# Where the weight buffers of an fp32r matmul kernel begin, modulo 256 bytes

## What is computed

```python
# first block
mx = silu(c) @ ada_w + ada_b                      # modulation; the same for ctx
hx, hc = modulate(rmsnorm(x)), modulate(rmsnorm(ctx))
ux, uc = hx @ w_in, hc @ w_in                     # 1024 x 5120
ox = hgrn_bidir(ux, states from uc)               # gated scans in two directions
y = (sigmoid(..)*(fourier_mix(ux) @ w_a) + sigmoid(..)*(readout(ox) @ w_b)) @ w_out
x = x + mx2 * y
x = x + mx5 * ((silu(conv(h2 @ ffn_up)[:2816]) * conv(..)[2816:]) @ ffn_down)
# second block
p = rms_norm(x) @ w_in_2                          # 1024 x 2560
x = x + concat(band attention, short conv, pooling) @ w_out_2
x = x + square(relu(rms_norm(x) @ w_mlp1)) @ w_mlp2   # 1024 x 4096 and back
```

## Time and profile before

| | |
|---|---|
| median of 3 executions | 764.5 us (764.06 to 765.53) |
| profiled execution, device time | 764.52 us |
| its span, first to last instruction | 762.5 us |
| TensorE busy | 739.1 us, 97% of the span |
| VectorE / GpSimd / ScalarE busy | 491.2 / 398.5 / 358.6 us |
| mean granted TensorE clock | 0.993 |

### The profile page before, as it was taken

One profiled execution on the slowest core, in us unless ns is written; L12 is line 12 of the kernel. 1 busy time (PEld: TensorE's weight loads), 2 busy tenths in 40 slices (PEclk: granted clock), 3 DMA queues, 4 the chain that ended last, 5 costly groups with the idle time before them and its releaser, 6 DMA issues.

```text
span 762.5 us, 14142 instructions
## 1 busy us (share of the span) xinstructions
PE 739.1 (97%) x5852; PEld 717.0 (94%) x5852; DVE 491.2 (64%) x907; ACT 358.6 (47%) x452; POOL 398.5 (52%) x223
## 2 busy tenths in 40 slices
PE   7779999999999989999999999999899999999998
PEld 3679889999999989999999999999899999999997
DVE  3877797569526559777777764548655656556553
ACT  5586224245434555554555546346454433334331
POOL 0767553546648957878878877766585300000000
PEclk9999999999999989999999999999999999999999
DMA  9984886337534437555455544433435464464411
GB/s 362 417 360 162 344 304 262 140 111 244 207 110 159 166 117 294 177 188 200 167 170 199 184 167 166 166 112 111 148 133 203 181 220 165 169 216 160 176 57 56
DMA packets 21089, 145.84 MB, mean 191 GB/s; under 512 B 2465, under 2 KB 2977, under 8 KB 3746
## 3 DMA queue, kind: packets, MB, share of 16 engines
q1 hardware_dynamic: 20880, 144.87, 51.8%
q10 hardware_dynamic: 146, 0.07, 0.0%
HBM read 143.88 MB, written 1.05 MB: 190 GB/s over the span
## 4 chain that ended last, share of the span: by engine, by line
PE 90%; DVE 4%; ACT 4%; issue 2%; DMA 0%; DVEq 0%; ACTq 0%
PE bank L1426 24%; PE bank L1428 24%; PE bank L1427 24%; PE bank L1444 3%; PE CP L1428 2%; PE CP L1426 2%; PE CP L1427 2%; PE bank L1533 2%; PE bank L1469 1%; ACT SCR L793 1%; ACT whi L487 1%; PE bank L1484 1%; DVE GA L1119 1%; PE CP L1458 0%; PE bank L1642 0%
## 5 line engine op out<-in xcount | busy, mean ns | idle before, releaser
L469 POOL TENSOR_TENSOR wlo<-raw,whi 128x512 fp32r<-128x512 f32 (+1 forms) x201 | 377.8, 1910 | 170.6 <-ACT whi L487 170.5
L487 ACT ACTIVATE whi<-raw 128x2048 fp32r<-128x2048 f32 x103 | 196.3, 1907 | 43.7 <-PE bank L1428 29.2
L1186 DVE SCALAR_TENSOR_TENSOR Y<-bank,vec,Y 128x189 f32<-128x189 f32 (+2 forms) x352 | 123.0, 423 | 43.6 <-ACT Y L734 43.6
L1426 PE MATMUL bank<-H2h,whi 128*128 128x256 f32 x352 | 101.0, 287 | 1.7 <-DVE H2l L1161 1.7
L1427 PE MATMUL bank<-H2l,whi 128*128 128x256 f32 x352 | 100.6, 286 | 0.0
L1428 PE MATMUL bank<-H2h,wlo 128*128 128x256 f32 x352 | 99.8, 284 | 0.0
L1426 PE MATMUL bank<-H1h,whi 128*128 128x256 f32 (+1 forms) x288 | 90.9, 316 | 8.3 <-DVE H1l L917 4.5
L1428 PE MATMUL bank<-H1h,wlo 128*128 128x256 f32 (+1 forms) x288 | 89.2, 310 | 0.0
L1427 PE MATMUL bank<-H1l,whi 128*128 128x256 f32 (+1 forms) x288 | 89.0, 309 | 0.0
L850 DVE TENSOR_TENSOR wlo<-raw,whi 128x2048 fp32r<-128x2048 f32 x28 | 64.4, 2300 | 34.5 <-ACT whi L487 34.5
L1426 PE MATMUL bank<-H4h,whi 128*128 128x256 f32 x256 | 72.6, 284 | 0.0
(11 more groups left out here) (326 smaller groups left out, 1878.9 us busy)
## 6 DMA issues: line engine op xcount, KB each, us to landing
raw<-in_w_mlp SPq DMA_DIRECT2D x32, 1024.0 KB, 4.8
raw<-in_w_in SPq DMA_DIRECT2D x30, 1024.0 KB, 5.7
raw<-in_ffn_up SPq DMA_DIRECT2D x22, 1024.0 KB, 4.9
raw<-in_ada_hi SPq DMA_DIRECT2D x16, 1024.0 KB, 4.9
raw<-in_ffn_down SPq DMA_DIRECT2D x11, 1024.0 KB, 4.8
raw<-in_w_out SPq DMA_DIRECT2D x8, 1024.0 KB, 4.8
ada_s<-in_ada_s SPq DMA_DIRECT2D x4, 1024.0 KB, 18.1
ada_p<-in_ada_p SPq DMA_DIRECT2D x2, 1024.0 KB, 10.2
```

What stands on the lines that cost most here:

```text
L469: m = e.tensor_tensor(l[:, a:a + step], r[:, a:a + step], h[:, a:a + step].bitcast(F32), ALU.subtract)
L487: e.activation(whi[q % NHI][:, :], raw[n % NRAW][:, :], ACT.Copy).then_inc(s["w_hi"], 1)
L1186: e.scalar_tensor_tensor(o[:, r0:r1, c0:c1], z[:, r0 + dr:r1 + dr, c0 + dc:c1 + dc], cw[:, f, tap:tap + 1], o[:, r0:r1, c0:c1], ALU.mult, ...
L1426: e.matmul(out, h[:, col:col + P], xh, start=first, stop=False, skip_group_check=True)
```

## The change

`keep` gets a `lead`, a number of bytes left empty in front of a tile, and remembers where each tile lies. The three `whi` get leads of 192, 128 and 160 bytes, the three `wlo` leads of 224, 128 and 160. `base` is rounded up to a multiple of 1024. The tiles that borrow a weight buffer's space before it is first used (`ada_p`, `CROW`, `SQI`) are placed by the remembered offset instead of by the index. Nothing else differs: the instructions, their order on every engine and all semaphores are the same.

```diff
     start = 16512
     cursor = [start]
+    found = {}
...
-    def keep(name, shape, dt=F32):
+    def keep(name, shape, dt=F32, lead=0):
         size = int(np.prod(shape[1:])) * (1 if dt == U8 else 4)
+        cursor[0] += lead
+        found[name] = cursor[0]
         t = put(name, shape, dt, cursor[0])
...
-    whi = [keep(f"whi{i}", [P, CH], F32R) for i in range(NHI)]
-    wlo = [keep(f"wlo{i}", [P, CH], F32R) for i in range(NHI)]
+    whi = [keep(f"whi{i}", [P, CH], F32R, lead=(192, 128, 160)[i]) for i in range(NHI)]
+    wlo = [keep(f"wlo{i}", [P, CH], F32R, lead=(224, 128, 160)[i]) for i in range(NHI)]
...
-    base = cursor[0]
+    base = (cursor[0] + 1023) // 1024 * 1024
...
-    def at(t):
-        return (start + [*raw, *whi, *wlo].index(t) * CH * 4 - base) / 1024
+    def at(name):
+        return (found[name] - base) / 1024
...
-    CROW = area("CROW", [1, D], at(wlo[0]))
-    SQI = area("SQI", [P, KT, T], at(whi[2]))
+    CROW = area("CROW", [1, D], at("wlo0"))
+    SQI = area("SQI", [P, KT, T], at("whi2"))
```

More of the change, by code:

```diff
@@ L250, in build @@
     CBX = area("CBX", [P, D], 44)
-    def at(t):
-        return (start + [*raw, *whi, *wlo].index(t) * CH * 4 - base) / 1024
+    def at(name):
+        return (found[name] - base) / 1024
     ada_buf = {}
     for name, i, kb in (("ada_s", 0, 80), ("ada_s", 1, 48), ("ada_s", 2, 56), ("ada_s", 3, 88), ("ada_t", 2, 8),
-                        ("ada_t", 3, 24), ("ada_p", 0, at(whi[1])), ("ada_p", 1, at(wlo[2]))):
+                        ("ada_t", 3, 24), ("ada_p", 0, at("whi1")), ("ada_p", 1, at("wlo2"))):
         ada_buf[name, i] = area(f"{name}{i}", [P, CH], kb)
-    CROW = area("CROW", [1, D], at(wlo[0]))
-    SQI = area("SQI", [P, KT, T], at(whi[2]))
+    CROW = area("CROW", [1, D], at("wlo0"))
+    SQI = area("SQI", [P, KT, T], at("whi2"))
     TOK = area("TOK", [P, 2, D], 72)
```

## The result

The changed kernel takes 753.8 us (median of 4, 752.8 to 757.3), the kernel before 764.65 us beside it (764.1 to 765.5). The ratio is 0.9864 [0.9835, 0.9892]: faster by 1.4%, or 10.8 us, where 25.5 us were forecast. The direction was right, the forecast size more than twice what was measured, and, as the experiments show, the cause that I gave was wrong.

The account below looks back on a forecast made before the run. TensorE's start-to-start pace of matmuls was taken to bound the kernel. 764.5 us less 27.9 plus 1.4 and 1.0 gave 739 us, with 726 to 752 for this case and 724 to 778 for 8 in 10.

Parts of the forecast that it names:

- What bounds the kernel: Whole kernel: TensorE busy 97%, so the start-to-start distance of matmuls sets the time, whatever other engines do in SBUF.
- My reading: Matmul operands: a moving run beginning 32 past a multiple of 64 bytes costs 6.7 ns, such a load some 4 ns.
- The first rival: Matmul operands: weight-to-activation distance sets the pace and the new distances are worse; 775 us, from 767 to 786; chance 0.25.
- Pairs 0 and 1: Matmuls on the first two whi/wlo weight buffer pairs: aligned moving runs save 6.7 ns on 3168 matmuls, 21.2 us less.
- Pair 2: Matmuls on the third whi/wlo pair: load now 32 past a multiple of 64; 1584 matmuls, 4.3 us less.
- The 192 matmuls of 512 columns: Matmuls with two moving runs: 13.3 ns less for 143, 9.3 ns less for 49, together 2.4 us less.
- `by_tokens`: Its 288 matmuls, which load activations: 0.8 us less on pairs 0 and 1, 0.9 us more on pair 2, together nothing.
- The 1.4 us lost at the start: From 20 to 60 us, DMA engines 94% busy: at most 1.4 us of the gain does not arrive.
- The 1.0 us of the convolution: VectorE's convolution in the FFN stage: 1 us of waits at the stage's start, 3 us as the bad end.
- The holes: Empty bytes before weights, with XR, `con` and `vec` shifted: cost 0, with 1 us either way as bounds.
- The third: Matmul operands: distance matters and is better, one or two pairs falling; 757 us, from 750 to 762; chance 0.13.
- The second: Matmul pace: nothing changes with placement; 764.5 us, within 1 us; chance 0.20.

Follow-up runs that it names:

- e9: Changed kernel with weight-to-activation distances of 64 bytes on pairs 0 and 2 and 192 on pair 1; 745.8 us, 0.9758 of the kernel before.
- run 32: Not a follow-up run: words from "a moving run 32 past a multiple of 64", a stretch of moving operand beginning 32 bytes past such a multiple; no time.
- e1: Changed kernel with the six weight buffers and all activations 32 bytes lower, distances kept; 755.5 us.
- e2: Changed kernel with activations on a multiple of 1024 and all weight-to-activation distances back at 96 bytes; 765.15 us over 10 executions.
- e5: Changed kernel with all pairs at a weight-to-activation distance of 192 bytes; 756 us, executions from 748.9 to 759.7.
- e10: Changed kernel with weight-to-activation distances of 96 bytes in the FFN and second MLP and 192 in all other stages; 772.3 us.
- e12: Changed kernel with the distances of pairs 0 and 1 exchanged: 64, 192 and 160 bytes on pairs 0, 1 and 2; 751.8 us.
- e11: Changed kernel with weight-to-activation distances of 192 bytes on pairs 0 and 2 and 64 on pair 1; total time not given, FFN at 117.8, then 113.3 ns.
- e3: Changed kernel with weight-to-activation distances of 0, 32 and 128 bytes on pairs 0, 1 and 2; total time not given, paces 120.0, 116.7 and 118.8 ns.

## Where the prediction was right and which step failed

**What bounds the kernel: right.** Placement alone, with no instruction moved, took 2.4% off the time in e9, and the pace did not depend on the other engines.

**"My reading", the step that failed.** It took 6.7 ns for a moving run 32 past a multiple of 64 and 4 ns for a load. e1 and e2 give 0 for both with 256 columns: e1 puts the moving runs of all pairs 32 past such a multiple again and keeps the paces of 117.8 and 117.3 ns, e2 takes them off it and stays at 120.0. The evidence was the earlier trace rows against the earlier trace rows: 117.3 against 120.0 ns. I put that down to which operand was misaligned. It was the distance: 160 with the roles swapped, 96 without. The first rival's text had this very reading ("the loaded operand stands 96 bytes behind the moving one instead of in front of it"), and I set it aside because the excess grows with 512 columns. That argument was bad: no row showed how long a load reads beside the moving operand, and with 512 columns the pace follows the distance too, from 226.7 to 234.3 ns.

**The terms.** Pairs 0 and 1 were booked at 6.7 ns less, 21.2 us. They ran at 113.3 in stretches ahead of the FFN, but at 117.8 in the long stages: 2.2 ns, 7.0 us over the 3168 matmuls. Pair 2 at 117.3 came out to the tenth (4.3 us), which was luck: the reason given had nothing to do with it. The sum of the two, 11.3 us, is close to the 10.8 measured, but that is in part chance too, since in the trace only 7.1 us came in the long stages and the others gained and lost. The 192 matmuls of 512 columns (144 on pairs 0 and 1 and 48 on pair 2, not 143 and 49) were to run at about 220 and 224 ns and give 2.4 us; they ran at 233.3, 228.9 and 234.3 and gave 0.2. `by_tokens` at "113 on pairs 0 and 1 and over 125 on pair 2" was 117.8 or 113.3, and 120.0.

**The take-backs.** The 1.4 us lost at the start arrived as forecast or worse: the time to the first matmul of 512 columns did not fall at all. The 1.0 us of the convolution did not come: TensorE's only wait on VectorE in the FFN, for H2l, is 1.7 us in both kernels. The missing term was what the short stages take back: in the execution shown, 3.4 us of lower clock in `w_in_2`. With more matmuls at 113.3 ns more was taken back, in e5 by waits in `w_out`'s stage and behind GpSimd's split too, and e5 fell 19 us short of its own 731 to 737. Its trace is of its fastest execution, 748.9 us, and the clock does not separate that one from the slower ones: one of 758.1 us has the same mean granted clock, 0.988. What separates these two by 9 us is open.

**The holes: right.** e2 gives 0 within 0.1%. The larger base was not run by itself; e10's FFN shows no cost for it.

**The rivals.** The first had the mechanism and the wrong sign: no distance is above 120.0 with 256 columns (with 512, 160 is 1.0 ns above 96). 96, where the kernel stood before, is one of the two slowest places for 256 columns, so any other had to be as good or better, which no row of before could tell. The third ("distance, and better", 750 to 762, chance 0.13) holds the time and the mechanism, with all three pairs falling and not one or two. The second is refuted by the pace. Here the measurement and the Trainium skill differ: its page "TensorE: Matmul & The Clock Gate", section "Part 2: What happens when you issue a matmul", gives the moving operand and the load a read port each, neither taking from the other; the runs show up to 6.7 ns a matmul that depend on the distance of the two addresses. The Trainium skill's page "SBUF — State Buffer", section "SBUF: two separate sides", tells of lines of 16 bytes; what repeats here repeats with 256. The measurement decides.

## What to carry to other kernels

Where matmuls run back to back with a load each, print the address of every moving operand less that of its loaded one, modulo 256, and try two or three distances before arguing about alignment; it costs a few hundred bytes and no instruction. Choose it for the long stretches that TensorE bounds, and read the short stages apart: there a faster pace can become a wait, and time at the lower clock can take more than the pace gave. A pace found in one stretch is not safe in the next, so judge by counts in long windows of every stage.

## What had not been expected of the hardware

- The pace of float32r matmuls with a load each depends on the distance modulo 256 between their two operands: 113.3 to 120.0 ns with 256 columns, 226.7 to 234.3 with 512. The two forms do not rank alike: distance 0 is slowest for 256 (120.0, with 96) and fastest for 512 (226.7). The modulus is read from the table, where distances 128 bytes apart differ (116.7 and 117.3 at 32 and 160, 120.0 and 118.3 at 96 and 224) and buffers that agree modulo 256 alone, as the two `whi` at 64 in e9, share a pace.
- At distances 64 and 192 there are two steady paces, 113.3 and 117.8 ns, and at 160 there are 117.3 and 120.0 (e12). One is kept over many chunks and can change at a chunk's boundary, without a gap (e11 at 298.2 us). What repeats every 256 bytes, and what picks the pace, stays open; no run here looks inside the array's reads.
- GpSimd's split in four pieces took 5.9 to 6.0 or 8.0 us, its last piece 1.7 to 1.8 or 3.3 us by whether VectorE's own split of 2.5 us had begun 0.3 us before it; VectorE's square of 512 columns took 1.6 to 1.8 or 0.7 to 1.5 us. In e5 the profile named ScalarE's copy for a wait that ended 0.1 us after GpSimd did. This is read from fourteen traces; no experiment moved one of the two engines alone.
- Most changed versions spread more: 764.1 to 765.5 us before, 748.9 to 759.7 in e5, but 744.4 to 746.6 in e9. Why is not shown. The lower clock level came right behind TensorE's wait of 2.4 us in e5, and not behind those of 2.7 and 2.6 us at the same place in e3 and e10; the wait of 2.8 to 3.4 us in `w_in_2` is in all fourteen traces, the lower clock there in eight.
